# The core of a bidirectional gated DeltaNet: cross decays by a biased Exp, two row buffers, and two of four small copies on ScalarE

## The reference

```python
g = jnp.cumsum(chunks(g), axis=-1)
decay = jnp.exp(jnp.where(incl, g[..., :, None] - g[..., None, :], -jnp.inf))
k_beta = k * beta[..., None]
lower = jnp.where(strict, jnp.einsum('nbhid,nbhjd->nbhij', k_beta, k) * decay, 0.0)
rhs = jnp.concatenate([v * beta[..., None], k_beta * jnp.exp(g)[..., None]], axis=-1)
sol = lax.linalg.triangular_solve(eye + lower, rhs, left_side=True, lower=True)
a_qk = jnp.einsum('nbhid,nbhjd->nbhij', q, k) * decay
...
o = o_f + o_b
o = rmsnorm(o, norm_w) * jax.nn.silu(z)
return o.reshape(B, T, V_DIM) @ out_w
```

## Time and profile before

| | us |
|---|---|
| median of 3 runs | 3083.04 (3077.22 to 3084.6) |
| the profiled execution | 3080.21 |
| its span, first to last instruction | 3078.6 |
| busy: PE, DVE, ACT, POOL | 2871.2, 2188.6, 1259.3, 160.5 |
| TensorE's mean granted clock (share of full) | 0.966 |

### The profile page before, as it was taken

How to read it: one execution, slowest core, us unless ns; L and a number is a source line. 1 busy time by engine, 2 the same in 40 slices (tenths; PEclk the granted TensorE clock), 3 DMA queues, 4 the chain that set the end, 5 groups by cost and what they waited for, 6 DMA issues and landing times.

```text
span 3078.6 us, 38591 instructions
## 1 busy us (share of the span) xinstructions
PE 2871.2 (93%) x14244; PEld 2272.7 (74%) x14244; DVE 2188.6 (71%) x2273; ACT 1259.3 (41%) x1381; POOL 160.5 (5%) x303
## 2 busy tenths in 40 slices
PE   1799999998889989999999998999798999999998
PEld 1678888876665868888888887444677888888886
DVE  7599989886982858877778785099857565555555
ACT  2356644335872444333333333300345333333333
POOL 0011211122110000000000000000000000000000
PEclk8799999999999989999999998999899999999998
DMA  9877787666654949878788884444156655556663
GB/s 400 281 255 279 281 296 253 198 219 195 197 151 171 389 171 352 330 290 337 297 311 333 322 338 172 137 151 146 66 185 238 213 204 204 204 203 204 213 204 118
DMA packets 322176, 731.66 MB, mean 238 GB/s; under 512 B 48128, under 2 KB 64336, under 8 KB 293648
## 3 DMA queue, kind: packets, MB, share of 16 engines
q1 hardware_dynamic: 316256, 709.85, 65.1%
q0 software_dynamic: 5808, 20.35, 1.9%
HBM read 710.45 MB, written 19.69 MB: 237 GB/s over the span
## 4 chain that ended last, share of the span: by engine, by line
PE 82%; DVE 8%; ACT 4%; DMA 3%; issue 2%; DVEq 0%; SPq 0%; POOL 0%; ACTq 0%; POOLq 0%
PE psg L707 45%; PE psg L713 22%; PE psg L694 7%; DMA aring<-in_ada_w 2%; DVE wlo L1149 2%; PE psn L1002 1%; PE psn L734 1%; PE pst L684 1%; DVE cv L1373 1%; ACT dec L2008 1%; PE psn L1112 1%; DVE y L1668 1%; ACT rv L2048 1%; DVE aacc L1248 1%; PE psn L684 1%
## 5 line engine op out<-in xcount | busy, mean ns | idle before, releaser
L1792 ACT ACTIVATE whi<-wraw 128x2048 fp32r<-128x2048 f32 x400 | 766.3, 1916 | 1216.9 <-PE psg L713 1103.5
L1149 DVE TENSOR_TENSOR wlo<-wraw,whi 128x2048 fp32r<-128x2048 f32 x400 | 917.6, 2294 | 475.8 <-ACT whi L1792 473.7
L707 PE MATMUL psg<-whi,h_hi 128*128 128x512 f32 x2304 | 731.4, 399 | 23.1 <-DVE h_lo L1748 13.2
L707 PE MATMUL psg<-whi,h_lo 128*128 128x512 f32 x2304 | 720.1, 394 | 0.0
L713 PE MATMUL psg<-wlo,h_hi 128*128 128x512 f32 x2304 | 570.9, 390 | 7.8 <-DVE wlo L1149 7.8
L707 PEld LDWEIGHTS psg<-whi,h_hi 128*128 128x128 f32 x2304 | 435.3, 191 | 116.6 <-issue 25.7
L707 PEld LDWEIGHTS psg<-whi,h_lo 128*128 128x128 f32 x2304 | 439.7, 191 | 93.9
L713 PEld LDWEIGHTS psg<-wlo,h_hi 128*128 128x128 f32 x2304 | 432.7, 188 | 99.3 <-DVE wlo L1149 9.3
L1159 DVE SCALAR_TENSOR_TENSOR aacc<-aring,cond,aacc 128x2048 f32<-128x2048 f32 x150 | 351.8, 2345 | 6.2 <-DMA aring<-in_ada_w 6.0
L694 PE MATMUL psg<-wraw,aring 128*128 128x512 f32 x512 | 221.1, 592 | 0.0
L707 PE MATMUL psg<-whi,g_hi 128*128 128x512 f32 x704 | 219.5, 393 | 0.0
(11 more groups left out here) (270 smaller groups left out, 2338.3 us busy)
## 6 DMA issues: line engine op xcount, KB each, us to landing
aring<-in_ada_w SPq DMA_DIRECT2D x192, 1024.0 KB, 6.9
wraw<-in_ffn_in_w SPq DMA_DIRECT2D x176, 1024.0 KB, 6.5
wraw<-in_gdn_in_w SPq DMA_DIRECT2D x96, 1024.0 KB, 5.2
wraw<-in_ffn_out_w SPq DMA_DIRECT2D x88, 1024.0 KB, 5.2
wraw<-in_cf_pw_w SPq DMA_DIRECT2D x48, 1024.0 KB, 5.2
wraw<-in_gdn_out_w SPq DMA_DIRECT2D x32, 1024.0 KB, 9.1
wraw<-d_rr SPq DMA_DIRECT2D x15, 1024.0 KB, 5.1
x<-in_x SPq DMA_DIRECT2D x2, 2048.0 KB, 8.8
```

The costliest lines, as they stand in the source:

```text
L707: mm(ps[:, t, 0:width], a[:, kc, t * P:(t + 1) * P], wh, start=first and j + n == 0, stop=False)
L1149: tt(wlo[:, j % 2, :], wraw[:, j % 4, :], whi[:, j % 2, :].bitcast(F32), SUB).then_inc(w_lo, 1)
L1792: av(whi[:, j % 2, :], wraw[:, j % 4, :], ACT.Copy).then_inc(w_hi, 1)
```

## The change

1. **Cross decays.** VectorE no longer makes segment 1; ScalarE makes it from the row itself, with the column of `ncum` as the bias of the Exp. Exp now takes two instructions for each c and kind: one for the two masked segments, one of 128 columns with a bias. Of kind 0, the 32 outer columns that nobody reads are left out in the Exp of the masked segments and in VectorE's product.
2. **Two row buffers.** `rr_even` beside the one in `wraw`; since ScalarE now reads the rows, a buffer is free when kind 1 of its head is done (`d1_done`) and no more when the sums are done (`ex_done`). `go_raw(1)`, which uses the odd buffer's place, moves behind `d1_done`.
3. **Layout.** `inv_b` moves into the place of `whi`, and POOL clears it before the last z slice is stored, with a wait for `w_used`. Other tiles of the core move.
4. **Early first decays.** The decays of head 0 (both kinds) and of head 1 (kind 0) stand on ScalarE ahead of the evacuation of the last z slice (a Silu); on VectorE the sums of head 1 stand ahead of `keys(0)`. On SP the q/k and rows of head 1 come ahead of the inverse of head 0, and the first output weights behind both inverses. The waits for `z_out` move back, as does TensorE's for `ps_read`.
5. **Two copies.** Of the four copies of t's result (`turned`) two move to ScalarE, between `oT` and `rv`; TensorE waits for both engines.
6. The first operation of the norm moves from VectorE to GpSimd.

```diff
@@ sync
             def core_loads(s):
 
                 if s + 2 < HQ:
-                    sp.wait_ge(ex_done, s + 2)
+                    sp.wait_ge(d1_done, s + 1)
                     load_rr(s + 2)
                 if s + 2 == HQ:
-                    sp.wait_ge(ex_done, HQ)
-                    go_raw(1)
                     sp.wait_ge(u1_done, 13)
                     go_raw(2)
+                if s + 1 == HQ:
+                    sp.wait_ge(d1_done, HQ)
+                    go_raw(1)
...
             store_inv()
-            load_w(G_GO, G_GO % 4, rows4(gdn_out, 0, 0))
-            sp.wait_ge(c_init, C_CONST + 1)
-            sp.wait_ge(inv_out0, 48)
-            load_inv(0)
             sp.wait_ge(kq_done, 1)
             load_qk(1)
             sp.wait_ge(w_lo, G_GO - 2)
             load_rr(1)
+            sp.wait_ge(c_init, C_CONST + 1)
+            sp.wait_ge(inv_out0, 48)
+            load_inv(0)
             sp.wait_ge(c_init, C_CONST + 3)
+            sp.wait_ge(inv_out, 48)
             load_inv(1)
+            load_w(G_GO, G_GO % 4, rows4(gdn_out, 0, 0))
@@ vector
                 for c in cs:
-                    for seg, t, kind, tj in ((0, 0, 0, 0), (2, 1, 0, 1), (1, 1 - c // 2, 1, c // 2)):
...
-                        if seg == 1:
-                            i = ts(to, row, col, 0.0, ADD, MIN)
-                        else:
-                            i = stt(to, row, col, tri0[:, c // 2:c // 2 + 1, :].broadcast_to([P, 2, P]), ADD, MIN)
+                    for t in range(TT):
+                        i = stt(exb[:, h % 2, c, :, t, :], rows_of(h)[:, 2 * c:2 * c + 2, t * P:(t + 1) * P], ncum[:, 0, t, c, h:h + 1],
+                                tri0[:, c // 2:c // 2 + 1, :].broadcast_to([P, 2, P]), ADD, MIN)
...
                 if A:
                     dve.wait_ge(t_done, s + 1)
-                    for d, b0 in QUADS:
+                    for d, b0 in QUADS[:2]:
                         (lead, rest), slot = halves(d, b0), slot_of(2 * d)
                         i = nc.vector.tensor_copy(turned[s][lead, slot:slot + 2, :, rest], ps_t[lead])
                     i.then_inc(t64_done, 1)
...
+            decay_sums(1, range(4))
             keys(0)
             queries(0)
@@ scalar
-            z_evac(7, 1)
-
-            act.wait_ge(kn_out, 16 * 16)
 
             def decays(h, kind, done):
 
                 for c in range(4):
-                    i = av(dec[:, h % 2, c, kind].rearrange("p s m -> p (s m)"),
-                           exb[:, h % 2, c, kind].rearrange("p s m -> p (s m)"), ACT.Exp)
+                    n = c // 2
+                    m0, m1 = (0, P) if kind else (32 * (1 - n), P - 32 * n)
+                    av(dec[h % 2][:, c, kind, 0:3:2, m0:m1], exb[:, h % 2, c, kind, :, m0:m1], ACT.Exp)
+                    i = av(dec[h % 2][:, c, kind, 1, :], rows_of(h)[:, 2 * c + kind, (1 - n) * P:(2 - n) * P], ACT.Exp,
+                           bias=ncum[:, 1, n, c, h:h + 1])
                 i.then_inc(done, 1)
...
+                if A:
+                    act.wait_ge(t_done, s + 1)
+                    for d, b0 in QUADS[2:]:
+                        (lead, rest), slot = halves(d, b0), slot_of(2 * d)
+                        i = av(turned[s][lead, slot:slot + 2, :, rest], ps_t[lead], ACT.Copy)
+                    i.then_inc(t64a_done, 1)
...
-                if M:
+                if M and s:
                     act.wait_ge(ex_done, s + 2)
-                    if s:
-                        act.wait_ge(x_done, s)
+                    act.wait_ge(x_done, s)
                     decays(s + 1, 0, d0_done)
...
+            act.wait_ge(kn_out, 16 * 16)
+            act.wait_ge(kk_out, 16 * 4 * 4)
             act.wait_ge(ex_done, 1)
             decays(0, 0, d0_done)
             decays(0, 1, d1_done)
-            act.wait_ge(z_out, 16 * NZ)
             act.wait_ge(inv_out0, 48)
             act.wait_ge(inv_out, 48)
-            act.wait_ge(kk_out, 16 * 4 * 4)
+            act.wait_ge(ex_done, 2)
+            decays(1, 0, d0_done)
+            z_evac(7, 1)
@@ gpsimd
             pool.wait_ge(w_lo, G_GO - 1)
             pr.inc(ms(inv_a[:, :, :, :], 0.0))
-            store_z(7, 1)
             pool.wait_ge(w_lo, G_GO)
             pr.inc(ms(inv_c[:, :, :, :], 0.0))
-            pool.wait_ge(inv_out0, 48)
-            pool.wait_ge(inv_out, 48)
+            pool.wait_ge(w_used, G_GO - 1)
             pr.inc(ms(inv_b[:, :, :, :], 0.0))
+            store_z(7, 1)
```

More of the change, by code:

```diff
@@ L119, in build @@
         wraw = sb("wraw", [P, 4, TILE])
+        core_st = ExitStack()
+        core_whi = sb("core_whi", [P, 2, 8, TT, P], at=core_st)
+        core_st.close()
         whi = sb("whi", [P, 2, TILE], F32R)
@@ L216, in build, with rows_of @@
         inv_at = tuple(128 * inv_of[:h + 1].count(inv_of[h]) for h in range(HQ))
+        def rows_of(h):
+            return rr_odd if h % 2 else rr_even
         oT = sb("oT", [P, HV, T], at=p2a)
@@ L337, in build @@
         inv_out0, inv_out = sem("inv_out0"), sem("inv_out")
-        qk_land, rr_land, v_land, z_land = (sem(n) for n in ("qk_land", "rr_land", "v_land", "z_land"))
+        qk_land, v_land, z_land = (sem(n) for n in ("qk_land", "v_land", "z_land"))
+        rr_land = [sem(f"rr_land{i}") for i in range(2)]
+        om_done = sem("om_done")
         inv_land = [sem(f"inv_land{i}") for i in range(3)]
@@ L345, in build @@
         aq_done = sem("aq_done")
-        w_done, wt_done, t_done, t64_done = (sem(n) for n in ("w_done", "wt_done", "t_done", "t64_done"))
+        w_done, wt_done, t_done, t64_done, t64a_done = (sem(n) for n in ("w_done", "wt_done", "t_done", "t64_done", "t64a_done"))
         rv_done = sem("rv_done")
@@ L931, in step @@
                     for c in range(4):
-                        i = mm(ps_a[:, c, :], dec[:, q, c, 0, 1, :], uu[:, 0, c, :], start=True, stop=True)
+                        i = mm(ps_a[:, c, :], dec[q][:, c, 0, 1, :], uu[:, 0, c, :], start=True, stop=True)
                     i.then_inc(x_done, 1)
@@ L954, in step @@
                 if M:
+                    if s == 0:
+                        pe.wait_ge(ps_read, S_GO)
                     pe.wait_ge(qk_land, 32 * (s + 2))
@@ L1464, in decayed @@
                 kqf = kqs if h else kq0
+                skip = 32 * (1 - kind)
                 for d in range(2):
                     n = 2 - 2 * d
-                    f = dec[:, h % 2, 2 * d:2 * d + 2, kind].rearrange("p c s m -> p c (s m)")
-                    for to, kq in ((f[:, :, d * P:(d + 2) * P], kqf[:, d, kind, :]),
-                                   (f[:, :, n * P:(n + 1) * P], kqf[:, 1 - d, kind, (1 - d) * P:(2 - d) * P])):
+                    lead, tail = (skip, 0) if d == 0 else (0, skip)
+                    f = dec[h % 2][:, 2 * d:2 * d + 2, kind].rearrange("p c s m -> p c (s m)")
+                    for to, kq in ((f[:, :, d * P + lead:(d + 2) * P - tail], kqf[:, d, kind, lead:2 * P - tail]),
+                                   (f[:, :, n * P + lead:(n + 1) * P - tail], kqf[:, 1 - d, kind, (1 - d) * P + lead:(2 - d) * P - tail])):
                         i = tt(to, to, kq.unsqueeze(1).broadcast_to(list(to.shape)), MUL)
@@ L2027, in step @@
                         act.wait_ge(og_done, g)
+                    else:
+                        act.wait_ge(z_out, 16 * NZ)
                     av(os[:, :, :], ps_o, ACT.Copy, scale=float(P) ** -0.5).then_inc(oc_ok, 1)
@@ L2333, in _ @@
             for h in range(2, HQ + 2):
-                pool.wait_ge(oms_done, 2 * (h - 2) + 2)
                 m, r, a = (oms[:, n, :] for n in (1, 2, 3))
+                pool.wait_ge(osq_done, h - 1)
+                if h > 2:
+                    nr.wait(pool)
+                    pool.wait_ge(og_done, h - 2)
+                nc.gpsimd.tensor_scalar(m, oms[:, 0, :], 1.0 / P, RMS_EPS, MUL, ADD).then_inc(om_done, 1)
+                pool.wait_ge(oms_done, h - 1)
                 for _ in range(3):
```

46 lines of the change are left out of this document (21 added, 25 removed).

## The result

The changed kernel takes 3122.86 us (median of 4 runs, 3112.73 to 3123.9), the kernel before 3082.22 (now over 4 runs): a ratio of 1.0127, 95% interval 1.0106 to 1.0149. It is slower, as forecast, but by 40 us and not by 15, and outside the range. The profiled execution took 3123.9 us, its span is 3122.3.

The account below looks back on a forecast made before the run. It took the ScalarE-TensorE chain of waits to bound each core step. Start -4.3, thirteen steps +24.0 and end -2.6 sum to +17.1 us: 3097.3 or 3100.1 by base, given as 3098.5, range 3087 to 3110.

Parts of the forecast that it names:

- The loop: Core step: ScalarE's work from kind 1's first Exp to `yb`, plus 3.6 us of TensorE; 12.73 becomes 14.58 us.
- what left VectorE: Core step: about 1.6 us of work leaving VectorE hides in its wait for ScalarE and gains nothing in steady steps.
- The rival that had ScalarE's wait take up the new work: Core step: VectorE was the bound, ScalarE's 2.1 us wait absorbs the added 1.85; 3065.5 us, chance 0.08.
- Exp: Cross decays on ScalarE in each core step: kind 1 +0.74 and kind 0 +0.53, together +1.27 us.
- three rows lie on the line: Reason given for taking Exp at +1.27 us a step, between bounds of +0.95 and +2.3.
- The copies: Two copies of t's result on ScalarE between `oT` and `rv`: +0.58 us a step, between 0.34 and 0.67.
- The clock: Rival, t2 and O in core steps: TensorE's clock falls in the thinner step; +13 to +23 us, about 3116, chance 0.10.
- The start: Core start up to O of step 1: reordered first decays, with rows landing 5.1 us after issue, give -4.3 us.
- The end: Step 15: the last inverse loads sooner, TensorE's 3.55 us wait goes, step 12.3 us; -2.6, between 0 and -3.

Follow-up runs that it names:

- the doubled products: The changed kernel with both u products (u0 and u1) made twice by TensorE in each step: 3104.2 us, ratio 1.0070 to the kernel before.

## Why the prediction was wrong, step by step

**The loop** was right. ScalarE and TensorE alone set the step, and what left VectorE bought nothing: it is busy 9.46 us in the changed kernel's step, for 11.90 before, and the quiet step is longer by just what ScalarE's chain got. The rival that had ScalarE's wait take up the new work fell: the wait stayed at 2.10 us in the quiet step, as forecast.

**Exp** was right, 1.27 for 1.27, but not for the reason given, "three rows lie on the line". The line goes through two points, 0.20 at 128 columns and 0.413 at 384, and gives 0.306 at 256. The two rows at 256 columns lie below it: `yb` at 0.28, and 0.367 less 0.09 for the pointer, also 0.28. By those, kind 1 would have come to +0.64 and not +0.74. That the line held (0.31 and 0.25 from start to start were measured) was in part luck.

**The copies** were mis-sized, 0.85 instead of 0.58 a step. Their own time was right (0.58 for two). What was left out is that nothing overlaps `oT` any more when a copy follows it, 0.12, and another 0.12 ahead of `yb`, whose cause stays open. The forecast's own row of line 2065, "one after the other without overlap", hinted at the first, and the forecast counted the tail of `oT`, 0.09, only in the upper bound. In thirteen steps it is 3.5 us. That the copies don't overlap because they are on part of the partitions is likely from these rows, and no run tried it.

**The clock** is the step that failed. It stood as a rival, "TensorE's clock falls in the thinner step", with +13 to +23 us and "about 3116", and it was given 0.10. The sum put this term at nothing. It happened, and at the rival's size: about 14 us in the thirteen steps and 1.6 in step 15. The reason given against it was a stretch with TensorE busy 68% at a clock of 1.00, against 75% here. That row was a single step, with its idle behind a run of full steps; the changed kernel has 2.31 and 1.35 us of idle in every step. One row at the high level doesn't show that a repeated step keeps it, and the same rows had the other answer, 0.65 in a stretch with TensorE busy 74%. With both rows weighed alike the chance should have been near one half, and the range would have had to reach to the upper end of that rival, 3121. Even that is 2 us short, since the start and the end gave less and the copies cost more than forecast.

**The start** was forecast at -4.3 and came out at -0.3, reckoned from the key/query product. Head 1's rows landed 8.3 us after that product's end and not 6.2: the issue came 1.4 us after it, not 1.1, and the load took 6.95 us and not 5.1. Head 1's sums and kind 0, `ev` and `wtc` hung on it. The median of 15 loads of the steady steps stood for one at the start; in that stretch the inverse's stores and the weights moved too, but which of them slowed it wasn't tried. Up to the end of kind 1 this makes 2.5 of the 4.0 us. The other 1.5 lie in step 1; 0.9 of them are x, which took 2.08 us at a granted clock of 0.50 instead of the 1.16 of a steady step, and the rest I haven't traced. A low clock was priced in step 0's key/query product alone.

**The whole run ahead of the core** was 3.6 to 3.8 us later in the profile of the changed kernel. The code is the same there, and 2.1 of it is there already 180 us into the span. The other kernels of the study had the product end between 704.6 and 708.2, and with the doubled products, where all ahead of the core is the changed kernel's, it ended at 706.3 for 708.5 here. So most of it is what one execution differs from another; for the medians it says little.

**The end** was right in kind: no wait for the last inverse, 11.8 to 12.6 us for step 15 in the three kernels with an addition undone, for 12.3 forecast. In the changed kernel O's low clock took most of it back (14.3).

The sum with the measured terms: start -0.3, thirteen steps 13 x 2.12 = 27.5 and 13.8 for the clock, end -0.6, and 3.6 from before the core: +44.0, less 0.3 behind step 15, for 43.7 in the span. Against the forecast's +17.1 that is 13.8 for the clock, 4.0 for the start, 3.5 for the copies, 2.0 for the end (1.6 of it the clock again) and 3.3 outside the core.

## What to carry to other kernels

The busiest engine isn't the bound: read the chain of one step, and put work only on engines that aren't in it; here VectorE was busy 11.9 of 12.75 us and taking work from it bought nothing in a step. Where a change lengthens a step without giving TensorE more to do, price its low clock as a likely case and not as an accident, above all where TensorE waits twice in each step; an extra product in those waits tells within one run whether the clock is the cause. When an engine's loop is shortened, look for the loop that is next: here a loop of 12.77 us took the place of the one of 12.73, and the step didn't become shorter.

## What was not expected of the hardware

- TensorE's granted clock falls in a regular loop of small steps without one long wait: 2.31 and 1.35 us of idle in a step of 14.9 us gave 2.4 GHz in one step of three and 1.2 GHz under O in two (4.58 us instead of 2.94). A kernel with 1.7 us more matrix work in each step (TensorE busy 12.68 of 14.85 us for 10.95 of 14.90) ran 18.7 us faster. A step of 13.6 us showed it in no step, one of 13.1 us with 2.37 us of idle ahead of W in five of thirteen.
- Copies on ScalarE of 32 partitions by 128 columns cost 0.29 us each and don't overlap the instruction ahead of them: 0.59 us from `oT`'s start to the next, 0.47 without them.
- A switch between Exp and Silu costs 1.28 us by every row of before and after, and an instruction behind it that has nothing else to wait for starts 0.01 to 0.02 us later (722.52 + 1.28 = 723.80, `ev` at 723.82). The Trainium skill (ScalarE: Activation LUTs, What ACT_TABLE_LOAD costs) counts a drain of about the same size on top; the rows here don't show it, and the measurement decides.
